# Last stage of a hybrid decoder layer: row finishing, y turns and w_out steps moved to other places of a hand-written order

## The reference

```
y_pool = multiscale_pool(u_pool, pool_w, pool_scale) * silu(z_pool)     # (2048, 512)
y_attn = attn * silu(z_attn)                                            # (2048, 512)
gates  = sigmoid(gate_logits + b_gate)                                  # (2048, 2, 1024)
merged = gates[:, 0] * (y_pool @ w_pool_up) + gates[:, 1] * (y_attn @ w_attn_up)
x      = x + merged @ w_out
out    = rms_norm(x, final_g)
```

## Time and profile before

| what | value |
| --- | --- |
| median of 3 runs | 1619.43 us (1616.13 to 1619.94) |
| profiled execution, its own time | 1619.43 us |
| its span on the core | 1617.3 us |
| mean granted TensorE clock | 0.994 of full |
| busy: TensorE, VectorE, GpSimd, ScalarE | 97%, 77%, 62%, 48% |
| up products | about 1268 to 1453 us |
| output products | about 1453 us to the end |

### The profile page before, as it was taken

One profiled execution on the slowest core, in us unless ns is written; L12 is line 12 of the kernel. 1 busy time (PEld: TensorE's weight loads), 2 busy tenths in 40 slices (PEclk: granted clock), 3 DMA queues, 4 the chain that ended last, 5 costly groups with the idle time before them and its releaser, 6 DMA issues. The chain is left out here.

```text
span 1617.3 us, 24744 instructions
## 1 busy us (share of the span) xinstructions
PE 1566.8 (97%) x7934; PEld 1304.0 (81%) x7934; DVE 1242.7 (77%) x1646; ACT 782.6 (48%) x1500; POOL 1001.3 (62%) x713
## 2 busy tenths in 40 slices
PE   7999999999999999999999999999999999999997
PEld 6887888788888887888877878888888787778875
DVE  6745424774989889998988978889888646677888
ACT  4412222214666666666665666666666411123333
POOL 3421102421688878888777887788875243357886
PEclk9999999999999999999999999999999999999999
DMA  6633335755433342443694433334424587665443
GB/s 250 230 128 130 131 117 180 243 163 156 132 112 107 82 122 91 122 118 117 187 319 147 136 92 90 117 89 121 114 78 132 175 268 246 220 187 179 164 165 123
DMA packets 163936, 245.78 MB, mean 152 GB/s; under 512 B 47697, under 2 KB 80977, under 8 KB 163810
## 3 DMA queue, kind: packets, MB, share of 16 engines
q1 hardware_dynamic: 163810, 244.20, 48.2%
HBM read 158.15 MB, written 85.99 MB: 151 GB/s over the span
## 5 line engine op out<-in xcount | busy, mean ns | idle before, releaser
L1576 DVE TENSOR_TENSOR_SCAN left<-keep,left 128x512 f32<-128x512 f32 x192 | 298.8, 1556 | 33.3 <-issue 21.1
L1403 PE MATMUL psum<-hT,ring 128*128 128x512 f32 x644 | 264.7, 411 | 5.0 <-DVE sum_d L1612 2.4
L1643 POOL TENSOR_TENSOR ring<-raw,ring 128x512 fp32r<-128x512 f32 x138 | 233.3, 1690 | 58.6 <-ACT ring L1483 43.7
L1407 PE MATMUL psum<-hT,ring 128*128 128x512 f32 x644 | 263.2, 409 | 0.0
L1405 PE MATMUL psum<-hT,ring 128*128 128x512 f32 x644 | 262.5, 408 | 0.0
L1489 ACT ACTIVATE keep<-psum 128x512 f32<-128x512 f32 (+3 forms) x320 | 170.8, 534 | 178.8 <-PE psum L1429 176.4
L1496 ACT ACTIVATE wt<-psum 128x512 fp32r<-128x512 f32 (+3 forms) x320 | 171.2, 535 | 110.3 <-PE psum L1437 107.4
L1449 PEld LDWEIGHTS psum<-wt,vm 128*128 128x128 f32 x1088 | 171.5, 189 | 32.9 <-issue 7.0
L1582 DVE TENSOR_TENSOR wt<-psum,wt 128x512 fp32r<-128x512 f32 (+3 forms) x320 | 189.7, 593 | 8.4 <-ACT wt L1496 5.9
L1449 PE MATMUL psum<-wt,vm 128*128 128x256 f32 x1088 | 182.4, 282 | 5.1 <-DVE row_sum L1591 4.3
L1437 PE MATMUL psum<-ident,left 128*128 128x128 f32 x1088 | 170.8, 272 | 1.4 <-DVE wt L1582 1.3
(11 more groups left out here) (217 smaller groups left out, 3426.7 us busy)
## 6 DMA issues: line engine op xcount, KB each, us to landing
raw<-in_w_strips SPq DMA_DIRECT2D x92, 256.0 KB, 4.0
qm<-qk_scratch SPq DMA_DIRECT2D x128, 128.0 KB, 4.2
gate<-gate_scratch SPq DMA_DIRECT2D x64, 256.0 KB, 4.6
hT<-form_scratch SPq DMA_DIRECT2D x28, 512.0 KB, 8.6
xt<-in_x SPq DMA_DIRECT2D x16, 512.0 KB, 4.9
xT<-in_x_T SPq DMA_DIRECT2D x16, 512.0 KB, 3.8
qk_scratch<-staging SPq DMA_DIRECT2D x32, 256.0 KB, 2.6
qk_scratch<-store_lo SPq DMA_DIRECT2D x32, 256.0 KB, 3.4
```

The costliest lines, as they stand in the source:

```text
L1403: pe.matmul(o, hi, m_hi, start=k == 0, stop=False)
L1407: last = pe.matmul(o, lo, m_hi, start=False, stop=k == HK - 1)
L1576: dve.tensor_tensor_scan(left[:, n % LN, span][:, ::-1], k, k, carry, ALU.mult, ALU.bypass).then_inc(scanned, 1)
L1643: pool.tensor_tensor(out_, a, b, op).then_inc(s, 1)
```

## The change

Six places of the order in `stage4` are moved; no instruction of an engine is added or taken away, and nothing is computed otherwise.

1. `WO_FIRST` is at n = 16 instead of 20, so the loads of w_out come at n = 15, 23, 31 and 39.
2. The splits of the attention y are one a step, at m = 3, 4, 6 and 7, with GpSimd's `attend` one step ahead of each.
3. The splits of the pool y are at m = 2 to 5 instead of 4 to 7.
4. A weight piece is loaded one step later (3 steps ahead instead of 4).
5. z for k = 0, 1 is loaded behind the attention y of its own chunk instead of half a chunk earlier.
6. Row finishing: a pair's first square moves from step 6 to step 0 of the next pair and the second from 0 to 1; the means are at 1 and 2, the roots at 1 and 2 behind the rest of the step, `finish_row` at 2 and 3.

```diff
-    WO_FIRST, WO_STEPS = at_up(1, 0, 4), 8
+    WO_FIRST, WO_STEPS = at_up(1, 0, 0), 8
...
-    ATTEND = {3: (0, 1), 6: (2, 3)}
-    Y1_TURN = {4: (0, 1), 7: (2, 3)}
+    Y1_TURN = {3: 0, 4: 1, 6: 2, 7: 3}
...
@@ sync
-            load_up(EARLY)
             for n in range(UPS):
                 c, b, m = up_of(n)
-                if n + EARLY + 1 < 2 * NM:
-                    load_up(n + EARLY + 1)
+                if n + EARLY < 2 * NM:
+                    load_up(n + EARLY)
...
                 if m == 0 and b == 1 and c + 1 < NC:
                     sp.wait_ge(up_done, at_up(c, 1, 0))
                     opening.load_y(sp, 0, tokens(c + 1))
-                    load_z(c + 1, 0)
-                    load_z(c + 1, 1)
                 if m == 0 and b == 0 and c >= 1:
                     sp.wait_ge(up_done, at_up(c, 0, 0))
                     opening.load_y(sp, 1, tokens(c))
+                    load_z(c, 0)
+                    load_z(c, 1)
...
@@ scalar (vector has the same with _low)
-                if b == 0:
-                    for k in Y1_TURN.get(m, ()):
-                        y1_high(c, k)
-                if b == 1 and m >= NM - UK and c + 1 < NC:
-                    y0_high(c + 1, m - NM + UK)
+                if b == 0 and m in Y1_TURN:
+                    y1_high(c, Y1_TURN[m])
+                if b == 1 and 2 <= m < 2 + UK and c + 1 < NC:
+                    y0_high(c + 1, m - 2)
...
@@ scalar, output products
-                if p >= 1 and j == 0:
-                    root(p - 1, 0)
-                if p >= 1 and j == 2:
-                    root(p - 1, 1)
                 if s < PARTS and j in (A11, S1):
                     take(s)
                 if s + AHEAD < PARTS:
                     form_high(s + AHEAD)
-                if j == A22:
-                    square(p, 0)
-                if p >= 1 and j == 0:
-                    square(p - 1, 1)
+                if p >= 1 and j in (0, 1):
+                    square(p - 1, j)
+                if p >= 1 and j in (1, 2):
+                    root(p - 1, j - 1)
@@ vector, output products
-                if j == A22:
-                    row_mean(p, 0)
-                if p >= 1 and j == 0:
-                    finish_row(p - 1, 0)
-                if p >= 1 and j == 1:
-                    row_mean(p - 1, 1)
-                if p >= 1 and j == 3:
-                    finish_row(p - 1, 1)
+                if p >= 1 and j in (1, 2):
+                    row_mean(p - 1, j - 1)
+                if p >= 1 and j in (2, 3):
+                    finish_row(p - 1, j - 2)
@@ gpsimd
-                if b == 0:
-                    for k in ATTEND.get(m, ()):
-                        attend(c, k)
+                if b == 0 and m + 1 in Y1_TURN:
+                    attend(c, Y1_TURN[m + 1])
```

More of the change, by code:

```diff
@@ L2267, in _ @@
                     up_low(n + 2)
-                if b == 0:
[L2269 to L2272, removed]
+                if b == 0 and m in Y1_TURN:
+                    y1_low(c, Y1_TURN[m])
+                if b == 1 and 2 <= m < 2 + UK and c + 1 < NC:
+                    y0_low(c + 1, m - 2)
                 i = n - WO_FIRST
```

## The result

| | before | after |
| --- | --- | --- |
| median of 6 runs each | 1616.74 us | 1644.36 us (1639.99 to 1650.72) |
| ratio, 95% interval | | 1.0168 [1.0144, 1.0191] |
| profiled execution, span | 1617.3 us | 1641.4 us |
| up products, first matmul to the first of w_out's | 184.1 | 199.3 |
| output products, first to last matmul | 154.4 | 160.6 |

The change is slower by 1.68%, 27 us, where 11 were forecast (from 1619.43 to 1630): the direction was right, and the time lies above the range of eight in ten (1616 to 1637). The profiled spans differ by 24.1: 0.7 ahead of the up products, 15.2 in them (forecast -0.1), 8.2 behind them (forecast 11.3).

The account below looks back on a forecast made before the run. TensorE, busy 97%, bounds the kernel, with a VectorE and GpSimd loop pacing the output products. Up products -0.1 and output products +11.3 us give +11.2 on the 1617.3 span: 1630 forecast, own range 1624.5 to 1636, eight in ten 1616 to 1637.

Parts of the forecast that it names:

- six pairs: Output products: moving row finishing lengthens the VectorE and GpSimd loop from 19.74 to 21.15 us a pair, +8.4 us over six.
- tail: Output products, after the last join of sum_a: both finishes of pair 6 stand before sum_d, +4.1 us (3 to 5).
- Rival A: Output products: the loop is broken, pace becomes TensorE's 19.04 us, stops go (-2.0), tail costs 0; 1617.3 us, chance 0.12.
- sum_d ends before T+8.6: Output products: condition for the loop being broken, not lengthened; T is the start of the join of sum_a, times in us.
- rival C: Slower still: mt load misses its pair, 1 to 2 us in five pairs, or y waits a whole MB; 1636 to 1643, chance 0.08.
- -9.5 + 7.4 + 1.7 + 0.3 = -0.1: Up products, us: old stops and slow clock won, new chunk 1 and 2 stops, one clock fall, later weight pieces.
- One up piece less in flight: Up products: pieces issued one step, about 2.7 us, later; the last ready about 0.5 us before its product; 0.3 us.
- Chunk 3 has no w_out in front: Up products, chunk 3: y load no longer waits behind chunk 2's late multiplies, so stops of 2.86 and slow-clock 1.7 us go.
- 2.2 us more: Up products: next z load, behind a gate load awaiting the m = 3 multiply, waits longer for two w_out operations and that multiply.
- 3.7: Up products: stop in us in each of chunks 1 and 2, from y 1.5 later and z 2.2 later; 7.4 together.
- one fall, 1.7: Up products: TensorE's clock falls once in the two new pairs of stops, costing 1.7 us (0 to 3.4).
- both stops of 1.89 go: Up products, chunks 2 and 3: pool y turns at m = 2 to 5 remove both its stops, 1.89 us each.

## Why the prediction was right and wrong

**Row finishing: mechanism right, a bit too dear.** Shown by the part alone and by the PSUM runs: VectorE's scaling with two SBUF operands and GpSimd exclude each other, the finishes stand in front of sum_d, GpSimd runs dry (2.02 us) and the loop is longer. Term by term: the first interval -1.1 (forecast -1.2); six pairs 5.8 (8.4, 20.71 against 21.15 a pair); tail 3.55 (4.1). GpSimd's second half is what came quicker: from sum_d to the next add into sum_a ends 10.4 us, where the working has 10.7, and sum_d itself was 0.3 earlier. Rival A and its exit, "sum_d ends before T+8.6", are refuted by T+10.2. Of rival C the missed mt load didn't come (joins 20.71 apart, less than forecast), and y in chunk 1 was 1.9 us late and not the 4.5 of a whole megabyte; that 1644 lies just above its 1636 to 1643 is no support for it.

**Up products: the step that failed is the sum "-9.5 + 7.4 + 1.7 + 0.3 = -0.1"**, three of its terms:

- *"One up piece less in flight ... 0.3 (0 to 1.5)".* It measured 4.1 in the profile and 5.0 us alone. The queue was not followed: piece 12's issue falls from ahead of the 1 MB pool y to behind it. The prediction counted the step's 2.7 us and not what stands in front at the new place. Nearly half of the 4.1 is piece 15, for which the prediction named the gate load in front and had it only just in time. In the changed kernel this cost may not be on top of the others': with the pieces put back the one profile shows y stopping longer, and the ratio fell by 0.2%, within its interval.
- *"Chunk 3 has no w_out in front ... its 2.86 and 1.7 go."* The pool y's stop went and the attention y's came back, 3.5 + 1.5. The "2.2 us more" for a z load behind a gate load that waits for the multiply of m = 3 was seen, but put down for chunks 1 and 2 alone. Single turns make it hold in each chunk (a stop of 3.92 in chunk 3 with nothing else changed), z ahead of the gate load about halves it, and with turns and z put back chunk 3 loses nothing.
- *The clock.* "3.7" a chunk was near, 4.6 and 4.4 us; one fall, 1.7, was three, 7.0 us. In these runs a stop of 3 us or more and the slow matmuls behind it cost 5 to 8 us together.

The gate multiply's stop, 1.0, had no term. So 9.0 for 7.4 at the y of chunks 1 and 2, 3.5 for nothing in chunk 3, 7.0 for 1.7, 4.1 for 0.3 and this 1.0 make 24.6 in place of 9.4.

Two things held. "both stops of 1.89 go" did. And in chunk 1 the mechanism was right: forecast 1.5 us for y and 2.2 for z, measured 1.9 and 2.3, and with w_out back at its steps the chunk loses 1.2 in place of 7.5. For chunk 2 the blame on w_out isn't borne out: it stops with w_out ahead of y or not.

**What the parts add up to.** Alone they cost 0.54, 0.31, 0.52 and 0.04%, 1.41 together, against 1.68 in one. The intervals of the four make the sum uncertain by about 0.4 (root of the sum of squares), so an interaction beyond the sum isn't established by the times. The chunks show one: in chunk 1 w_out and pool y alone lose 1.2 us and turns and z alone 1.6, but the changed kernel 7.5 (9.3 with the pieces put back), and either put back leaves about 1. That is the most of why turns and z win 15 us of up products when put back last (6.6 in chunk 1, 5.0 in chunk 3, 3.1 in chunk 2) and cost some 7 to 9 alone. It rests on one profile of each run. Whether other costs replace each other is open: the two put-backs that left the up products at 200 have ratios 0.2% lower, within their intervals, and the pool y at m = 2 to 5 was not put back by itself.

## What to carry to other kernels

When a load is moved on a queue, list what stands in front of it at the new place and what engine's progress those issues wait for; the step's own length is the lesser part. A gain at one wait in a chain (pool y, attention y, pieces) is worth only what the next wait in it doesn't take back, so cost a stop with the clock that follows it. Where VectorE and GpSimd share SBUF work, look first for an operand that can live in PSUM: here that took away all 8 us that the moved order cost. The one reordering tried against the same exclusion, low halves behind the add in the kernel before, won nothing.

## What the runs showed of the hardware

- The scaling of 128 x 1024 took 1702 ns on average of sixteen with both tensors in SBUF (six beside GpSimd at 2.40 us, ten at 1.28), and 1284 ns with one in PSUM, whatever GpSimd did. The Trainium skill (SBUF — State Buffer, "SBUF: two separate sides") says that a VectorE instruction with two SBUF inputs and a GpSimd one that reads SBUF exclude each other, the loser blocked for the whole instruction; the trace agrees.
- Every stop of 3 us or more in the up products (3.03 to 5.02) was followed by 6 to 14 matmuls about 0.43 us apart, TensorE at 1.2 GHz. It isn't the length alone: with row finishing moved and the weights in PSUM, a single stop of 1.64 was followed by eight such steps and one of 2.45 by none, and one of 1.82 with z ahead of the gate load by none. In that first case the slow matmuls begin 1.8 us after the stop (1384.40 to 1386.20), not at it.
